# Squares in PSUM, later last rows and token sums, another slot order, first weights ahead of the seventh tile, and a 64-byte shift of the large tiles

## The reference, cut to what matters

```
def swiglu(h, w_gate, w_up, w_down):
    return (jax.nn.silu(h @ w_gate) * (h @ w_up)) @ w_down

x = x + 0.5 * swiglu(rmsnorm(x, ffn1_norm[l]), ...)   # n = 0 and 2; n = 1, 3 alike
x = x + (jax.nn.silu(h @ w_gate) * (h @ w_up)) @ w_down   # n = 4
```

## Time and profile before

| | |
|---|---|
| median of 3 runs | 2542.91 us (2541.54 to 2545.0) |
| the profiled execution, its own time | 2542.93 us |
| its span | 2541.1 us |
| TensorE busy | 2479.8 us (98%), 12336 matmuls |
| VectorE, ScalarE, GpSimd busy | 1609.5, 1068.0, 730.3 us |
| mean granted TensorE clock | 0.991 |
| HBM read | 225.36 MB, 90 GB/s over the span |
| chain that ended last | PE 91%, DVE 5%, ACT 2%, issue 1% |

### The profile page before, as it was taken

The page is one execution under the profiler, slowest core; times in us unless marked ns, Lnnn a source line. Parts: engine busy times, 40 slices in busy tenths (PEclk is TensorE's granted clock), DMA queues, the critical chain, the costliest instruction groups (busy, mean ns, idle before and its releaser), DMA issues.

```text
span 2541.1 us, 31390 instructions
## 1 busy us (share of the span) xinstructions
PE 2479.8 (98%) x12336; PEld 2024.2 (80%) x12336; DVE 1609.5 (63%) x2021; ACT 1068.0 (42%) x1695; POOL 730.3 (29%) x426
## 2 busy tenths in 40 slices
PE   8999999999999999999999999999999988999998
PEld 7887888778888788887887778887887766888787
DVE  8887427768887327886137668887326655788712
ACT  5554114655554215554015555554213564555410
POOL 1001665432000560002665531001664323000154
PEclk9999999999999999999999999999999999999999
DMA  4331222113322223231222112432233111233122
GB/s 176 114 117 67 91 91 75 59 42 108 116 86 97 84 91 125 92 124 64 95 93 65 59 51 105 143 107 76 83 100 125 59 34 42 95 113 118 65 91 75
DMA packets 52386, 229.49 MB, mean 90 GB/s; under 512 B 7184, under 2 KB 10128, under 8 KB 39056
## 3 DMA queue, kind: packets, MB, share of 16 engines
q1 hardware_dynamic: 50528, 225.66, 26.0%
q10 hardware_dynamic: 1712, 1.82, 0.2%
HBM read 225.36 MB, written 2.10 MB: 90 GB/s over the span
## 4 chain that ended last, share of the span: by engine, by line
PE 91%; DVE 5%; ACT 2%; issue 1%; DMA 0%; DVEq 0%; SPq 0%; ACTq 0%
PE bank L926 13%; PE bank L925 13%; PE bank L927 13%; PE bank L803 12%; PE bank L801 12%; PE bank L802 12%; PE bank L949 2%; PE bank L1036 2%; PE bank L1021 2%; PE bank L875 1%; PE bank L877 1%; PE bank L876 1%; PE bank L1005 1%; DVE rstd L2008 1%; PE bank L1006 1%
## 5 line engine op out<-in xcount | busy, mean ns | idle before, releaser
L756 POOL TENSOR_SCALAR wh<-raw 128x1024 fp32r<-128x1024 f32 x192 | 212.4, 1106 | 1770.7 <-PE bank L927 1128.2
L759 POOL TENSOR_TENSOR wl<-raw,wh 128x1024 fp32r<-128x1024 f32 x192 | 471.4, 2455 | 16.0
L801 PE MATMUL bank<-act_all,wh 128*128 128x512 f32 (+1 forms) x902 | 357.9, 397 | 3.1 <-POOL wl L759 3.1
L803 PE MATMUL bank<-act_all,wl 128*128 128x512 f32 (+1 forms) x902 | 351.8, 390 | 0.0
L802 PE MATMUL bank<-act_all,wh 128*128 128x512 f32 (+1 forms) x902 | 350.3, 388 | 0.0
L2028 DVE SCALAR_TENSOR_TENSOR x<-bank,x 128x512 f32<-128x512 f32 x63 | 43.3, 687 | 408.9 <-PE bank L803 408.8
L1522 ACT ACTIVATE wh<-rawa 128x1024 fp32r<-128x1024 f32 x135 | 143.2, 1061 | 169.4 <-PE bank L927 161.0
L925 PE MATMUL bank<-wh,ss 128*128 128x512 f32 x540 | 213.2, 395 | 0.0
L927 PE MATMUL bank<-wl,ss 128*128 128x512 f32 x540 | 212.8, 394 | 0.0
L926 PE MATMUL bank<-wh,ss 128*128 128x512 f32 x540 | 212.8, 394 | 0.0
L2089 DVE TENSOR_TENSOR wl<-rawa,wh 128x1024 fp32r<-128x1024 f32 x135 | 165.1, 1223 | 60.7 <-ACT wh L1522 60.7
(11 more groups left out here) (374 smaller groups left out, 5454.5 us busy)
## 6 DMA issues: line engine op xcount, KB each, us to landing
raw<-in_stream SPq DMA_DIRECT2D x192, 512.0 KB, 3.4
rawa<-in_gu SPq DMA_DIRECT2D x60, 1024.0 KB, 4.8
raw<-in_gu SPq DMA_DIRECT2D x40, 1024.0 KB, 4.8
raw<-in_gu_small SPq DMA_DIRECT2D x20, 512.0 KB, 3.4
x<-in_x SPq DMA_DIRECT2D x8, 256.0 KB, 6.0
w1k<-in_w1k SPq DMA_DIRECT2D x1, 2048.0 KB, 7.9
w1v_low<-in_w1v SPq DMA_DIRECT2D x1, 1024.0 KB, 5.5
w1v_high<-in_w1v SPq DMA_DIRECT2D x1, 1024.0 KB, 7.6
```

The costliest lines, as they stand in the source:

```text
L756: nc.gpsimd.tensor_scalar(wh[:, h % 2, :, :], src, 1.0, 1.0, ALU.mult, ALU.mult)\
L759: nc.gpsimd.tensor_tensor(wl[:, h % 2, :, :], src, wh[:, h % 2, :, :].bitcast(F32), ALU.subtract).then_inc(split_done, 1)
L801: mm = nc.tensor.matmul(bank, wh[:, slot, k, :], rh, start=start, stop=False)
L803: return nc.tensor.matmul(bank, wl[:, slot, k, :], rh, start=False, stop=stop)
```

## The change

Eight edits: squares go to PSUM banks (6 and 7 for n = 0, 0 and 1 else, tile 6 of a seam to the one `sqf` left), with a new wait of TensorE before its first product of n > 0; the token sums move behind small product 2; `slot_of` gives another order from g = 3 on, and the waits follow it (`slot_free`, and GpSimd's for the first two down units); the fourth small quarter is split later on both engines; `token_mean`, `token_scale` and two sums change places on VectorE; the silu and the second rows of the last chunk move behind tiles f = 7, 8 and 10; the first quarter of weights is split ahead of tile 6 in the seams of n = 1, 3 and 4 (for n = 2 the place stays); GpSimd's `xg` of n = 0 waits for VectorE's low parts; and `room` grows by 64 bytes, which moves all that is declared after it.

```diff
 def slot_of(g):
-    return (0, 2, 1)[g % 3]
+    return (0, 2, 1)[g] if g < 3 else (2, 1, 0)[g % 3]
+
+def slot_free(n, g):
+    return n * GU + max(j for j in range(g) if slot_of(j) == slot_of(g)) + 1
...
-        room = sb("room", [P, 8])
+        room = sb("room", [P, 24])
...
-        sqf = sb("sqf", [P, 3, T], at=under_low)
+        sqf = sb("sqf", [P, T], at=under_low)
...
-            return sqf[:, at % KT % 3, :] if at // KT in PREP else sq[:, at % 4, :]
+            if at // KT in PREP:
+                m = at % KT
+                return B[6 + m % 2][:, :] if at < KT else B[m % 2][:, :] if m < 6 else sqf[:, :]
+            return sq[:, at % 4, :]
...                                                      # GpSimd
-                        pool.wait_ge(gu_used, (DOWN_AT.index(u) + 1) * GU - 1)
+                        pool.wait_ge(gu_used, (DOWN_AT.index(u) + 1) * GU - 2)
                     if u - 1 in DOWN_AT:
-                        pool.wait_ge(gu_used, (DOWN_AT.index(u - 1) + 1) * GU - 2)
+                        pool.wait_ge(gu_used, (DOWN_AT.index(u - 1) + 1) * GU)
...
+            pool.wait_ge(a_lo, tile_mark(0, KT - 1))
             for m in range(KT):
                 pool.wait_ge(x_in[m], 16)
...                                                      # TensorE, first_products
+                        if n > 0 and i == 0 and a == 0:
+                            pe.wait_ge(sq_used, 4 + PREP[n] * 8 + 6)
...
-                    if i == 1:
+                    if i == 2:
                         token_sums_of(n)
...                                                      # ScalarE
-                act.wait_ge(sq_used, at + (2 if at // KT in PREP and 3 <= at % KT < KT - 1 else 1))
+                act.wait_ge(sq_used, at + (3 if at // KT in PREP and 2 <= at % KT < (KT - 1 if at < KT else 6) else 1))
...
-                    act.wait_ge(gu_used, n * GU + g - 2)
+                    act.wait_ge(gu_used, slot_free(n, g))
...
             def feed_forward(n):
-                high_weights(n, 0, 3)
+                if n == 0:
+                    high_weights(n, 0, 3)
                 high_sum(n, 0)
                 high_sum(n, 1)
+                if n > 0:
+                    high_weights(n, 0, 3)
                 high_weights(n, 1, 0, 0)
+                high_sum(n, 2)
                 root(PREP[n], rc)
-                high_sum(n, 2)
                 high_weights(n, 1, 0, 1)
...
-                high_act(n, 4)
-                high_act(n, 5)
-                second_silu(n, LAST)
-                for f in range(6, FT):
+                for f in range(4, FT):
                     high_act(n, f)
+                    if f == 7:
+                        second_silu(n, LAST)
...
             def seam(n, g):
                 for m in range(KT):
+                    if m == (7 if n == 2 else 6):
+                        high_weights(n, 0, 0)
                     if m == 7:
-                        high_weights(n, 0, 0)
                         high_weights(n, 0, 1)
                     tile_parts(n, m, g(m))
...                                                      # VectorE
             def feed_forward(n):
-                low_weights(n, 0, 3)
                 low_sum(n, 0)
                 sum_rows(n, 2)
+                if n > 0:
+                    low_weights(n, 0, 3)
                 low_sum(n, 1)
                 sum_weights(n, 1, 0, 0)
-                token_mean(n)
                 low_weights(n, 1, 0, 0)
                 sum_weights(n, 1, 0, 1)
+                sum_rows(n, 3)
+                token_mean(n)
+                low_sum(n, 2)
                 token_scale(n)
-                sum_rows(n, 3)
-                low_sum(n, 2)
                 low_weights(n, 1, 0, 1)
...
                 rows_first(n, LAST)
-                low_act(n, 4)
-                low_act(n, 5)
-                rows_second(n, LAST)
-                for f in range(6, FT):
+                for f in range(4, FT):
                     low_act(n, f)
+                    if f in (8, 10):
+                        rows_second(n, LAST, f // 2 - 4)
...                                                      # VectorE, n = 0
+            for m in range(KT):
+                add_squares(m, rstd, m == 0)
+            low_weights(0, 0, 3)
             sum_rows(0, 1)
             sum_rows(0, 0)
-            for m in range(KT):
-                add_squares(m, rstd, m == 0)
...                                                      # VectorE, seam
-                    if m == 7:
+                    if m == {2: 7, 4: 6}.get(n):
                         low_weights(n, 0, 0)
                     update(m, factor, bank(m), *done(m))
+                    if m == 6 and n in (1, 3):
+                        low_weights(n, 0, 0)
```

More of the change, by code:

```diff
@@ L2141, in rows_first, with rows_second @@
                     V.scalar_tensor_tensor(p, sq[:, t, :], nrc[:, t:t + 1], p, ALU.mult, ALU.mult).then_inc(p_done, 1)
[L2143 to L2148, removed]
+            def rows_second(n, c, t):
+                dve.wait_ge(silu_done, (n * CHUNKS + c) * 4 + 3 + t)
+                dve.wait_ge(combined, (n * LAST + c - 1) * 6 + 3 + t)
+                p = product_rows(c)[:, 2 + t, :]
+                V.scalar_tensor_tensor(p, sq[:, 2 + t, :], nrc[:, 2 + t:3 + t], p, ALU.mult, ALU.mult).then_inc(p_done, 1)
             def low_act(n, f):
@@ L2179, in feed_forward @@
                             else:
-                                rows_second(n, c - 1)
+                                rows_second(n, c - 1, 0)
+                                rows_second(n, c - 1, 1)
                         if h in (4, 5):
```

## The result

| | before | after |
|---|---|---|
| median of runs | 2543.67 us (2541.54 to 2545.0, 4 runs) | 2526.91 us (2526.03 to 2528.51, 4 runs) |
| span of the profiled execution | 2541.1 us | 2524.2 us |
| mean granted TensorE clock | 0.991 | 0.996 |

After over before is 0.9939 [0.9922, 0.9955]: 16.8 us faster, against a forecast of 40. The sign was right and the size was not; 2526.9 lies above the range (2489 to 2522).

A forecast was written before the change was run, and what follows sets the result against it. The prediction took TensorE, busy for 98% of the span, as the bound: its idle time, lower clock and matmul pace. Its terms, -19.6 - 9.5 - 1.0 + 1.4 - 11.4 = -40.1 against 2542.93, gave 2503 us, range 2489 to 2522.

The forecast's parts named there:

- part 5: Wide products: 64 more bytes in `room` bring matmuls from `wh` and `wl` from 233.3 to 228.3 ns, net -11.4 us.
- parts 1 to 3: Second rows moved back (-19.6 us), weights split earlier in the seams (-9.5), new order in chunk 0 (-1.0 and +1.4).
- The rows moved back: Start of down projections: TensorE's idle time goes, 2.6 us in each of five stages, lower clock in four: -19.6 us.
- the earlier unit: GpSimd's first down unit starts 2.8 us earlier; its wait of 0.62 goes, and 0.3 us is left of that.
- The seams: First weight quarter ahead of tile 6: -3.5 us into n = 1 and 3, -3.2 and clock -2.8 into n = 4: -9.5.
- Chunk 0: VectorE gets late: stalls of 1.85 and 1.65 us leave -1.0 of 4.9 at the start; n = 2 loses 1.4.
- Squares in PSUM: Additions take 0.69 us as from SBUF, squares 0.58 instead of 0.61, beside TensorE's units: 0.
- the shift helps the products and slows the rest: Rival for `room`'s 64 bytes: 4002 matmuls of down projections, mixers and output lose 4.6 ns each, +18.4: 2521 us; chance 0.13.
- The shift does nothing: Rival: the 64 bytes in `room` have no effect, leaving -28.7 us: 2514 us; chance 0.25.

The follow-up runs named there:

- room8: The changed kernel with the 64-byte shift alone undone (`room` back to 8 columns): 2520.84 us, 0.9909.
- before_room24: The kernel before with the 64-byte shift alone (`room` at 24 columns): 2548.21 us, 1.0016.
- before_room56: The kernel before with the large tiles 192 bytes further on (`room` at 56 columns) and nothing else: 2512.11 us, 0.9866.
- rows_early: The changed kernel with the silu and the last chunk's second rows back ahead of f = 6, all else kept: 2533.33 us, 0.9957.
- room56: The changed kernel with `room` at 56 columns, 128 bytes further than the change's own: 2487.97 us, 0.9773.
- room40: The changed kernel with `room` at 40 columns, its large tiles 64 bytes further on: 2521.75 us, 0.9908.
- quarter3_room8: The changed kernel with `room` at 8 columns and, for n = 0, the fourth small quarter split after the sums on both engines: 2518.8 us, 0.9892.
- lead32: The changed kernel with `room` at 56 columns and a 128-byte tile ahead of all others, distances kept: 2487.22 us, 0.977.

## Why the prediction was right in sign and wrong in size

Forecast -40.1, measured -16.9 in the span. 17.4 of the missing 23.2 are in part 5 (-11.4 forecast, +6.0 measured as after against room8), 5.8 in parts 1 to 3. The steps:

**1. The rows moved back: right, slightly too high.** In room8 the down projections are 10.7 shorter and the last bit of each wide stage 0.6 (3.0 in five); with the 4.3 that two slow paces cost (below) the part is worth 18.0, forecast 19.6. Per stage 2.3 in place of 2.6, and 1.6 for the clock in four stages, as forecast (1.65). That four stages had this gain is in part luck: with the same wait of 2.1 us the clock fell in two of five stages in before_room24 and before_room56. The 0.3 is the unit that GpSimd starts earlier: it removed its own wait, and a wait of 0.37 for VectorE took its place. The attribution was also too simple. I gave the earlier unit 0.3; rows_early shows that it alone cuts the wait from 2.10 to 1.27, and there the clock stayed up. The two edits overlap, and their sum is less than what each does by itself.

The row products lasted 3.30 us beside the subtraction, 2.61 when they met less of it, and 0.74 each without it. By the Trainium skill ("SBUF — State Buffer", section "SBUF: two separate sides") a VectorE instruction with two SBUF inputs and a GpSimd one that reads SBUF exclude each other; these three times agree.

**2. The seams: right.** From room8: -1.6 and -1.7 into n = 1 and n = 3 (forecast -1.75 each), -3.1 and -2.4 for n = 4 (forecast -3.2 and -2.8). TensorE's wait there is 1.58 where it was 4.82, which is 3.24 less and does not hang on the length of the mixer. Sum -8.8, forecast -9.5. In after itself, into n = 1 and 3, it is worth nothing, as part 5 put slower matmuls in front of it.

**3. Chunk 0: right in its mechanism.** Both new waits came, 1.51 and 1.76 where I had 1.85 and 1.65. The start and n = 0 gained about 2.0 (2.55 less the 0.6 counted above) instead of 1.0, and n = 2 lost 1.5 (forecast 1.4).

**4. Squares in PSUM: no cost is seen.** No wait of the added semaphore is in the list. This part was not tried by itself.

**5. The shift: the step that failed.** "One shift of 64 bytes can turn every mixed pair into a same-side pair." I had read from the rows that pairs on the same side of `room` run alike, and had made two classes of it, same side and mixed. What counts is a distance in bytes. Tiles on one side of `room` are a multiple of 256 bytes apart; mixed pairs were 64 off, and 64 more bytes made them 128 off, not 0. It took 192. The pace of the wide products stayed at 233.0 (forecast 228.3, -13.8; the wide stages of after are 1.3 shorter than in room8), and the matmuls that I had left out of the sum, those of down projections and mixers, got slower: from 228.9 to 232.4 where the down projections had the faster pace, from 229.0 to 233.1 in the mixers' products of `mh` with `wh`. Against room8 that is +1.6 and +4.6 in the table (3.7 of it in the two mixers that repeat well). The small products lost +0.9 (forecast +2.4).

What was read rightly is the direction: same-side pairs are the slow ones at 256 columns (120 ns, the slowest of all) and the fast ones at 512, and room56 gets more than the -11.4, since the right distance serves the down projections and the mixers too. Of its 31.3 us against room8, 19.9 are in the wide products, 11.9 in the down projections and 3.1 in the mixers, the small products give 2.8 back, and the rest is outside these stages.

The rival that comes nearest is "the shift helps the products and slows the rest", in its second half only: the rest slowed by 6.2 instead of 18.4 and the products gained 1.3 instead of 13.8. Its 2521 is 6 us from the result, and its count was short: the trace before has 4542 matmuls of 512 columns in the down projections, mixers and output (2574 from `act_all`, 1248 and 144 from `xh` and `xl`, 576 from `mh` and `ml`), not 4002. With them it would have been +20.9 and 2524, above the range that was to hold it. "The shift does nothing" is refused by before_room24, whose interval excludes 1, and by the paces of after against room8. Placement as such is settled by room56. The section of the Trainium skill named above says that on the engine side only the port pair makes anyone wait, and the prediction took from it that place has no effect. TensorE's pace does depend on where its tiles lie, 226.7 against 233.3 ns, so the measurement decides. Whether that is a wait for another engine, or TensorE's two reads of its own, no run here shows.

The remaining 4.3 of the miss is the pace of the down projections at a distance of 64 bytes, which takes one of two values, 228.9 or 233.3, for a whole stage. I saw it in the earlier trace rows and noted it only as a doubt about place. In room8 it was the slow one in three stages, before in one. I priced its end (2.4 us) in the range only on the side of the gain.

**What stays open.** Why a distance of 0 modulo 256 bytes is fast for 512 moving columns and slow for 256; why matmuls from `wx` in room40 are slow behind those from `wh`; and what chooses between the two paces at a distance of 64. At 0 no run showed a second pace in the down projections.

## What to carry to other kernels

Before you tune waits of a kernel whose TensorE is busy for 98%, measure the distance of matmul starts in each kind of product, and set it against where the stationary and the moving tile lie: four kernels with the distance a multiple of 256 bytes ran their wide products and down projections at 226.7 ns, the others ran the pairs across `room` at 228.9 to 234.1. A padding tile is the cheapest experiment there is; try several sizes, not one, since the effect is not in proportion to them. And time a layout edit apart from the edits of order: here it hid a quarter of their gain (6.0 of 22.9, and with it the whole of one edit in two of three seams).

## What the runs showed of the hardware

- The start-to-start distance of fp32r matmuls with 512 moving columns is 226.7 ns if all tiles of the sequence start at the same byte of 256 (the distances were 0 and 256 modulo 1024), and 228.9 to 234.1 at distances of 64 to 192. At 256 columns it is the other way: 120.0 at 0, 113.3 to 118.9 at 64, 128 and 192, and 117.7 to 119.8 at 96. For the kernel before, the right distance is worth 1.3% (0.9866 [0.9842, 0.9891]).
- The same instructions on the same addresses have two paces (228.9 and 233.3) at a distance of 64, stage by stage, and keep one through a stage.
- `wx` is at distance 0 to `ea` and `ss` in all kernels. Its first matmuls behind those from `wh` are slower where these are: before, 226 to 236 ns for the first five, then 227; in room40, 224 to 236 for the first ten. The mean of 228.3 mixes the two.
- An idle stretch does not decide by its length alone whether the clock falls. Those of 2.1 us, alike in five stages, were followed by a granted clock of 0.5 in four stages in before, and in two in before_room24 and before_room56. One of 1.54 (quarter3_room8) was, those of 1.51 and 1.76 in after were not. The one of 1.80 in the mixer before n = 4, alike in all kernels, was in room8 and lead32 and not in before and after. Those of 1.3 at the start of the down projections of rows_early never were.
